# One order of steps over nine token tiles of an attention block: where a tile's last heads and its closing steps stand against the next tile's first ones

## The reference

```
z = rmsnorm(h) @ w_in                       -> cq, ckv, krope, hq, hf, hi, hg
q = rope(rmsnorm(cq) @ w_uq)                8 heads of 64 + 32
s = (q_lat . ckv + q_rope . krope) * SM_SCALE,  chunk-causal mask
o = softmax(s) @ ckv, then w_uv             512 columns (MLA group)
S_t = diag(f_t) S_{t-1} + (1 - f_t) i_t^T,  o_t = S_t^T q_t      4 heads (HGRN2 group)
o_hg = rmsnorm(o_t) * silu(hg)              512 columns
h = h + concat(o_mla, o_hg) @ w_o
h = h + hier_moe(rmsnorm(h));  y = rmsnorm(h)
```

## Time and profile before

| | us |
|---|---|
| median of 3 runs (lowest, highest) | 1440.64 (1438.37, 1443.41) |
| profiled execution, its own time | 1443.98 |
| its span | 1442.0 |
| PE busy in the span | 1180.2 (82%) |
| DVE, ACT, POOL busy | 709.4, 513.3, 327.3 |
| mean granted clock of TensorE | 0.886 of full speed |

### The profile page before, as it was taken

The page is one execution under the profiler, slowest core; times in us unless marked ns, Lnnn a source line. Parts: engine busy times, 40 slices in busy tenths (PEclk is TensorE's granted clock), DMA queues, the critical chain, the costliest instruction groups (busy, mean ns, idle before and its releaser), DMA issues.

```text
span 1442.0 us, 17999 instructions
## 1 busy us (share of the span) xinstructions
PE 1180.2 (82%) x5738; PEld 908.9 (63%) x5738; DVE 709.4 (49%) x1312; ACT 513.3 (36%) x920; POOL 327.3 (23%) x297
## 2 busy tenths in 40 slices
PE   4999999479988988899999999940788998989920
PEld 3898899434757676575757585720566776777720
DVE  4321011254634545454445453441687777778837
ACT  3332121233111112222213232300677777777712
POOL 2101200100000000000000000005565666566546
PEclk9999999769686979989789999975899999999965
DMA  6230211540101201010101000002669686764268
GB/s 231 95 129 23 93 60 48 161 117 20 30 20 44 68 20 59 30 45 30 44 23 51 30 30 23 15 30 65 227 237 345 223 287 221 247 227 151 87 249 310
DMA packets 94042, 160.15 MB, mean 111 GB/s; under 512 B 13435, under 2 KB 62060, under 8 KB 93980
## 3 DMA queue, kind: packets, MB, share of 16 engines
q1 hardware_dynamic: 80460, 114.11, 23.3%
q0 software_dynamic: 12432, 43.14, 8.4%
q10 hardware_dynamic: 1088, 2.10, 0.4%
HBM read 171.69 MB, written 41.10 MB: 148 GB/s over the span
## 4 chain that ended last, share of the span: by engine, by line
PE 59%; issue 11%; DVE 10%; DMA 9%; ACT 6%; POOL 2%; SPq 1%; POOLq 0%; ACTq 0%; DVEq 0%
PE ps L893 9%; DMA below<-in_w 6%; PE ps L861 5%; PE ps L750 4%; PE ps L732 4%; PE ps L820 3%; PE ps L1847 3%; PE ps L1848 3%; PE ps L1849 3%; DVE low L1543 3%; PE ps L1842 2%; PE ps L1841 2%; PE ps L1843 2%; PE ps L792 2%; ACT high L1293 2%
## 5 line engine op out<-in xcount | busy, mean ns | idle before, releaser
L1543 DVE TENSOR_TENSOR low<-below,high 128x1024 fp32r<-128x1024 f32 x132 | 204.1, 1593 | 83.0 <-ACT high L1293 76.5
L1385 PE MATMUL ps<-high 128*128 128x512 f32 x396 | 163.5, 413 | 21.5 <-DVE low L1553 11.3
L1254 POOL TENSOR_TENSOR low<-below,high 128x1024 fp32r<-128x1024 f32 x66 | 152.6, 2332 | 120.3 <-ACT high L1314 120.3
L1717 POOL TENSOR_SCALAR arena<-arena 128x1 f32<-128x1 f32 (+4 forms) x38 | 11.2, 295 | 715.7 <-ACT arena L690 382.1
L517 ACT ACTIVATE arena<-ps 128x512 f32<-128x512 f32 (+7 forms) x109 | 56.9, 531 | 301.9 <-PE ps L732 301.7
L1293 ACT ACTIVATE high<-below 128x1024 fp32r<-128x1024 f32 x132 | 132.9, 1052 | 75.5 <-DMA below<-in_w 75.5
L1387 PE MATMUL ps<-high,low 128*128 128x512 f32 x396 | 157.8, 398 | 0.0
L1386 PE MATMUL ps<-low,high 128*128 128x512 f32 x396 | 157.2, 397 | 0.0
L732 PE MATMUL ps<-arena 128*128 128x128 f32 (+4 forms) x613 | 107.8, 306 | 37.7 <-DVE arena L930 23.8
L893 PE MATMUL ps<-arena 128*128 128x512 f32 (+1 forms) x288 | 125.7, 594 | 2.3 <-ACT arena L517 1.7
L732 PEld LDWEIGHTS ps<-arena 128*128 128x128 f32 (+4 forms) x613 | 84.1, 170 | 53.0 <-issue 32.1
(11 more groups left out here) (209 smaller groups left out, 2035.4 us busy)
## 6 DMA issues: line engine op xcount, KB each, us to landing
below<-in_w SPq DMA_DIRECT2D x264, 256.0 KB
below<-in_w POOLq DMA_DIRECT2D x66, 512.0 KB
y_dram<-arena SPq DMA_DIRECT2D x33, 512.0 KB
arena<-in_x_prompt SPq DMA_DIRECT2D x16, 512.0 KB
below<-in_w_in SPq DMA_DIRECT2D x12, 512.0 KB, 6.4
out<-arena SPq DMA_DIRECT2D x9, 512.0 KB, 5.1
arena<-in_w_o SPq DMA_DIRECT2D x1, 4096.0 KB, 16.9
h_dram<-arena SPq DMA_DIRECT2D x8, 512.0 KB, 2.6
```

The source lines that it names most:

```text
L1254: pool.tensor_tensor(w2_lo[s % UN][:, c], w2_in[:, c], w2_hi[s % UN][:, c].bitcast(F32), ALU.subtract).then_inc(s_w2lo, 1)
L1385: pe.matmul(out, x_hi, w_hi, start=start, stop=False)
L1543: dve.tensor_tensor(chunk(w13_lo[j], c), chunk(w13_in, c), chunk(w13_hi[j], c).bitcast(F32), ALU.subtract).then_inc(s_w13lo, 1)
```

## The change

```diff
-    for i in range(NT):
-        STEPS.append(("meta", i, 0))
+    for i in range(NT + 1):
+        nxt = i + 1 < NT
         for hd in range(MH):
-            STEPS.append(("score", i, hd))
...
-            if hd >= 2:
-                STEPS.append(("attn", i, hd - 2))
-        STEPS += [("attn", i, 6), ("attn", i, 7)]
-        if i + 1 < NT:
-            STEPS.append(("hk", i + 1, 0))
-        STEPS.append(("mpv", i, 0))
...
+            if i < NT:
+                if hd == 0:
+                    STEPS.append(("meta", i, 0))
+                STEPS.append(("score", i, hd))
+                if hd == 0 and i:
+                    STEPS += [("pm", i - 1, 0), ("hk", i, 0)]
+                if hd == 1 and i:
+                    STEPS.append(("ho", i, 0))
+                    if nxt:
+                        STEPS.append(("hs", i + 1, 0))
+                if hd == 2:
+                    STEPS.append(("hf", i, 0))
+            if i and hd == 2:
+                STEPS.append(("mix", i - 1, 0))
+            if i < NT and nxt:
+                STEPS += [("h", i + 1, r) for r in {2: [0], 3: [1], 4: [3]}.get(hd, [])]
+            side = {3: "wot", 4: "wo", 5: "sq", 6: "hn"}.get(hd)
             if i and side:
                 STEPS.append((side, i - 1, 0))
+            if i and hd == 7:
+                STEPS.append(("hnt", i - 1, 0))
+            if i < NT and nxt:
+                STEPS += [("h", i + 1, r) for r in {3: [2], 4: [4], 5: [5], 6: [6], 7: [7]}.get(hd, []) if r < rounds(i + 1)]
+                if hd == 5:
+                    STEPS.append(("q", i + 1, 0))
+                if hd == 7:
+                    STEPS.append(("qt", i + 1, 0))
+            a = i * MH + hd - 2
+            if 0 <= a < NT * MH:
+                STEPS.append(("attn",) + divmod(a, MH))
+            if i and hd == 1:
+                STEPS.append(("mpv", i - 1, 0))
+            if i and hd == 7:
+                STEPS.append(("rt", i - 1, 0))
...
-        if st[0] == "score" and st[2] >= 2:
+        if st[0] == "score" and st[1:] >= (0, 2):
...
     def s_wait_free(pe, st):
         if k >= 2:
             pe.wait_ge(s_srel[k % 2], k // 2)
+            kind, i, _ = S_ORDER[k - 2]
+            if kind == "ho":
+                pe.wait_ge(s_oc, i + 1)
...
-            if kind == "mpv":
+            if kind == "pm":
                 act.wait_ge(s_dm, i + 1)
                 act.activation(pm_row[0:R], pm_row[0:R], ACT.Exp).then_inc(s_pm, 1)
-                evacuate(act, "act", st)
...
                     dve.wait_ge(s_sps2, k + 1)
-                    dve.wait_ge(s_oc, i + 1)
...
+            if kind == "mix":
+                sm = sm_stat[0:R, i % 2]
                 dve.wait_ge(s_pm, i + 1)
```

More of the change, by code:

```diff
@@ L216, in hybrid_layer @@
     pm_row = r.take(MH, META)
-    meta_row = r.take(MH, META)
+    meta_row = r.take(2 * MH, META)
     nbias = r.take(2, MH)
-    sm_stat = r.take(6, MH)
+    sm_stat = r.take(2, 5, MH)
     h_base = r.at
@@ L389, in hybrid_layer @@
     STEPS += [("vm", 0, 0), ("q", 0, 0), ("ho", 0, 0), ("hm", 0, 0), ("hs", 1, 0), ("qt", 0, 0)]
-    for i in range(NT):
-        STEPS.append(("meta", i, 0))
+    for i in range(NT + 1):
+        nxt = i + 1 < NT
         for hd in range(MH):
-            STEPS.append(("score", i, hd))
-            side = {1: "wot", 2: "wo", 3: "sq", 4: "hn", 5: "hnt", 6: "rt"}.get(hd)
-            if hd == 0:
-                STEPS.append(("hf", i, 0))
+            if i == NT and hd == 0:
+                STEPS += [("pm", i - 1, 0)]
+            if i < NT:
[15 more added lines that the diff above has]
+            side = {3: "wot", 4: "wo", 5: "sq", 6: "hn"}.get(hd)
@@ L414, in hybrid_layer @@
-    STEPS += [(s, NT - 1, 0) for s in ("wot", "wo", "sq", "hn", "hnt", "rt")]
+            if i and hd == 7:
[7 more added lines that the diff above has]
+            a = i * MH + hd - 2
@@ L450, in hybrid_layer @@
             P_INDEX[st + (0,)] = len(P_INDEX)
+    S_ORDER = list(S_JOB)
     def last_group(a):
@@ L668, in attention_act @@
             R = ROWS[t]
-            if kind != "mpv":
-                evacuate(act, "act", st)
+            evacuate(act, "act", st)
             if st in S_JOB:
@@ L708, in attention_act @@
                                    bias=nbias[0:R, i % 2, hd:hd + 1], scale=SCALE,
-                                   accum_out=sm_stat[0:R, 2, hd:hd + 1]).then_inc(s_srel[k % 2], 1)
-            if kind == "mpv":
+                                   accum_out=sm_stat[0:R, i % 2, 2, hd:hd + 1]).then_inc(s_srel[k % 2], 1)
+            if kind == "pm":
                 act.wait_ge(s_dm, i + 1)
                 act.activation(pm_row[0:R], pm_row[0:R], ACT.Exp).then_inc(s_pm, 1)
-                evacuate(act, "act", st)
             if kind == "sq":
@@ L943, in attention_dve @@
             R = ROWS[t]
-            if kind != "mpv":
-                evacuate(dve, "dve", st)
+            evacuate(dve, "dve", st)
             if kind == "hs":
@@ L1035, in attention_dve @@
                         dve.wait_ge(s_b7done, B7_JOB[("meta", i, 0)] + 1)
-                        if i:
-                            dve.wait_ge(s_dm, i)
-                        dve.tensor_copy(meta_row[0:R], ps[0:R, 7, 0:MH * META].rearrange("p (h m) -> p h m", h=MH)
+                        mrow = meta_row[0:R, MH * (i % 2):MH * (i % 2) + MH, :]
+                        dve.tensor_copy(mrow, ps[0:R, 7, 0:MH * META].rearrange("p (h m) -> p h m", h=MH)
                                         ).then_inc(s_b7free, 1)
@@ L1041, in attention_dve @@
                         if t == LAST:
-                            link(dve.memset(meta_row[0:SAMPLE], NEG))
-                        dve.tensor_reduce(sm_stat[0:R, 1, :], meta_row[0:R], AX.X, ALU.max)
+                            link(dve.memset(mrow[0:SAMPLE], NEG))
+                        dve.tensor_reduce(sm_stat[0:R, i % 2, 1, :], mrow, AX.X, ALU.max)
                     dve.wait_ge(s_sps2, k + 1)
@@ L1050, in attention_dve @@
                         link(dve.memset(S[0:64, w - 64:w], NEG))
-                    link(dve.tensor_reduce(sm_stat[0:R, 0, hd:hd + 1], S[0:R, 0:w], AX.X, ALU.max))
-                    dve.tensor_scalar(nbias[0:R, i % 2, hd:hd + 1], sm_stat[0:R, 0, hd:hd + 1],
-                                      sm_stat[0:R, 1, hd:hd + 1], -SCALE, ALU.max, ALU.mult).then_inc(s_nb, 1)
+                    link(dve.tensor_reduce(sm_stat[0:R, i % 2, 0, hd:hd + 1], S[0:R, 0:w], AX.X, ALU.max))
+                    dve.tensor_scalar(nbias[0:R, i % 2, hd:hd + 1], sm_stat[0:R, i % 2, 0, hd:hd + 1],
+                                      sm_stat[0:R, i % 2, 1, hd:hd + 1], -SCALE, ALU.max, ALU.mult).then_inc(s_nb, 1)
                 if kind == "wo":
@@ L1062, in attention_dve @@
                                       ALU.add).then_inc(rel, 1)
-            if kind == "mpv":
-                mrow = meta_row[0:R]
+            if kind == "pm":
+                mrow = meta_row[0:R, MH * (i % 2):MH * (i % 2) + MH, :]
                 dve.wait_ge(s_nb, (i + 1) * MH)
@@ L1068, in attention_dve @@
                                          op0=ALU.mult, op1=ALU.add).then_inc(s_dm, 1)
+            if kind == "mix":
+                sm = sm_stat[0:R, i % 2]
                 dve.wait_ge(s_pm, i + 1)
                 s_wait_read(dve, ("score", i, MH - 1))
[L1071 to L1075, removed]
+                link(dve.tensor_reduce(sm[:, 3, :], pm_row[0:R], AX.X, ALU.add))
+                link(dve.tensor_tensor(sm[:, 3, :], sm[:, 3, :], sm[:, 2, :], ALU.add))
+                link(dve.reciprocal(sm[:, 4, :], sm[:, 3, :]))
+                dve.wait_ge(s_pused, P_INDEX[("mpv", i, 0, 0)] + 1)
                 dve.tensor_tensor(mix_row[0:R, :].rearrange("p (h v) -> p h v", h=MH),
                                   ps[0:R, 6, :].rearrange("p (h v) -> p h v", h=MH),
-                                  sm_stat[0:R, 4, :].unsqueeze(2).to_broadcast([R, MH, VD]), ALU.mult
+                                  sm[:, 4, :].unsqueeze(2).to_broadcast([R, MH, VD]), ALU.mult
                                   ).then_inc(s_mix, 1)
```

## The result

The changed kernel takes 1460.39 us (median of 4 runs, 1455.28 to 1461.99) against 1439.51 us (4 runs): ratio 1.0134, 95% interval 1.0102 to 1.0167. I had forecast 1431 with a range to 1452. The result lies on the other side of no change, and beyond the range.

A forecast was written before the change was run, and what follows sets the result against it. PE was taken to bound the attention: work at the upper clock, the lower clock's price, and waiting. Walked at full clock -22 us, +12 for the lower clock, +0.5, makes -10: forecast 1431 us, range 1412 to 1452.

The forecast's parts named there:

- The walked waits: PE's new waits in the attention, walked at full clock for i = 7 (9.8 us) and i = 3 (some 12).
- the mix: At i = 7 the new tile's first product waits 2.7 us for s_mix, behind score2, hf and the sums on DVE.
- `attn7`'s copy: attn7's product waits for DVE's copy, 2.0 us at i = 7, or ACT's behind the squares, 1.8 at i = 3.
- bank 7: At i = 3, h'1 waits 2.9 us for this bank, because DVE frees it behind hf and mix.
- `h'2`: This round waits for DVE's h'1, which stands behind score3: 1.7 us at i = 7; 1.5 at i = 3.
- step 3: After ho at i = 7: DVE's state, hs' and attn7 first-group copy take 3.1 us, cover 1.1, wait 2.0.
- `ho` for the first exponential: At i = 3, ho waits 1.6 us for head 0's exponential, which holds its slot, behind pm and hk on ACT.
- `hk`'s bank: At i = 7, the second group of attn6 waits 1.8 us for the bank that ACT's copy of hk frees.
- What the lower clock will cost: Attention: 12 us, between 0 and 22; two waits a tile cost 5 us of slower work, 3.5 of it absorbed.
- the first tile: Its rounds begin two heads later: +1 us, called small.
- the long runs of transposes: attn5 to attn7 held the clock down for 20 us and more in narrow tiles; scores and ho break them up.
- The third: Rival: rt and meta back to back ahead of score0 keep the clock down through ho; +36 us, 1455 us, chance 0.26.

The follow-up runs named there:

- qt_early: Kernel before with one step moved, the next tile's qt ahead of attn6 and attn7: 1405.5 us, ratio 0.9763 to before.
- mix_and_pm: Changed kernel with mix directly behind mpv and pm behind the tile's last maxima: 1437.7 us, ratio 0.9993 to before.
- mpv_spread: Order of qt_early in the changed kernel's code, pm behind attn5, mpv between attn6 and attn7, its last products and mix behind hk: 1392.6 us, ratio 0.9659 to before.
- experiment 1: Changed kernel with the router product rt moved from ahead of meta to behind mpv in the tile after: 1458.9 us, ratio 1.0126 to before.
- Experiment 7: qt_early with a wait put back at meta, for ACT's copy of ho, ACT's squares or POOL's power: 1425.7, 1437.8 and 1453.2 us.
- score0_ahead: mpv_spread with the next tile's meta and score0 moved ahead of this tile's attn7: 1437.7 us, ratio 1.0005 to before.

## Why the prediction was wrong

**Right: what goes and what comes.** The wait of meta went. The walked waits came, in place and roughly in size: the mix 2.7 forecast, 2.39 in tile i = 7 (2.1 to 3.4 in the four wide tiles); `attn7`'s copy 2.0 and 1.8, measured 1.2 to 2.0 (0.4 in the last tile); bank 7 in the narrow tiles 2.9, measured 2.2 to 2.6 (in the fourth 1.2); `h'2` 1.7, measured 0.5 to 1.4. Two sums of the walk were loose: the waits listed for i = 3 add up to 13.0 us ("some 12"), and the chain of step 3 to 2.9 ("3.1"); neither changes the forecast by more than 4 us. Too large were those that a PE at the lower clock reaches late: `ho` for the first exponential (1.6, once 0.8) and `hk`'s bank (1.8, at most 0.95).

**The step that failed: "What the lower clock will cost ... I take 12".** At full clock the walk gave -22 us for the tiles. The stretch came out at +15.9. That leaves 38 us for the lower clock and the first tile where the sum had 12 + 0.5. About 29 of them are the term that I had put at 12. My 12 was eight tiles of 5 us of slower work less 3.5 us that the waits absorb, so 40 less 28. What the windows give for the same two parts, as an estimate: PE is busy for 477 us in the eight windows with 411 us of work at full clock (my 417, less the 6 us done earlier), so 66 us of slower work; the walk had 93 us of waiting at full clock (510 less 417) and 56 are idle, so 37 absorbed. The waits absorbed somewhat more than I took. The slower work did not: it was 67 us before and stayed there, where I had it fall to 40.

I had argued that the long runs of transposes held the clock down and that breaking them up frees it. In sum nothing was freed: the busy time of the stretch is 524.6 us against 521.9. In the narrow tiles the breaking up may have helped (i = 2 went from 0.81 to 0.94), and the wide ones gave it back. From tile i = 4 on the runs were not the cause: in `qt_early` the runs of `attn5` to `attn7` stand as before, `qt` among them, and from 569 us to the end of the last `attn` the clock falls once, for 3 us. What frees it there is that the wait ahead of meta is gone: one put back at the same place brings back some 20 of the 29 us of busy time, in each of three profiles. The changed kernel has two or three waits of over 1 us in each tile's start but the last's. That each of them has such a price is argued from this; the runs that took some of them out got back less than meta's price (`mix_and_pm`: 12.0 us of idle and 5.3 us of busy time). Why the first two tiles are at the lower level for most of their time in every order, `mpv_spread` too (0.71 from 361 to 440 us), no run shows.

**Also mis-sized: the first tile.** I gave "+1" for its rounds beginning later. From the first meta record to the first product of meta probabilities it takes 53.9 us against 39.0 (360.19 to 399.22). Some 6 us of this is work that the new order does earlier; the rest, about 9, is loss: idle 8.6 us instead of 3.5, at a clock of 0.69.

**The rivals.** The third ("the lower clock through the tile's start", 1455) had the side, and with 36 us nearly the size. Its cause, `rt` and `meta` back to back, found no support: with `rt` elsewhere nothing was gained (experiment 1). That its time came close is luck. It should have been put on the waits, of which I had already counted more than before. Seen from the rule of the Trainium skill that I had weighed ("TensorE: Matmul & The Clock Gate", "HAM oscillation — how this bites in real kernels"), reading it as the forecast would have given the right side. The section behind it, "A second HAM failure mode: psum-queue depth-cycling", fits these runs closer: it says that short idle moments between groups of matmuls, if frequent, make the clock go up and down as well. Its case is a bf16 kernel with 512 columns. Experiment 7 agrees in part: eight waits of 0.7 us cost 19 us of busy time in the profiled execution, and three of four executions paid about that. Frequent they are not, one in each tile of 57 to 70 us.

**What the forecast hid.** The change does two things. The queries' move is worth 34 us (`qt_early` against before, 1405.5 and 1439.5). The rest, `hk`, `ho`, `mpv` and `mix` under the next tile, costs 55 (1460.4 less 1405.5); no single run makes this step alone, so it is a difference and not a measurement. In a sum of waits at full clock the two looked like -22; neither waits alone nor the clock alone give their sizes.

**Open.** Why the step in busy time sits at this place is not settled: `qt_early` keeps waits of 1.0 us at round 0 and of up to 1.7 us in narrow tiles with much of its time at full clock, while 0.7 us directly ahead of meta costs 19 us. Nor is it meta alone. `qt_early` waits 0.75 us ahead of `mpv`'s product (L745) in all the tiles from the second on, and in three of them the product's two records then run at the lower level, as here:

```profile
763.75 2.08 PE L745 MATMUL ps<-arena 128*128 128x512 f32 x2 [0.75 <-DVE arena L551]
```

In four others they take 1.13 us behind the same wait. `mpv_spread`, in which these waits are covered, has no lower stretch from 498 us on. So the same wait at the same place has a price at one time and none at another, and what decides it these runs do not show. That the 16-column products of meta matter is an idea that no run here tests apart.

## What to carry to other kernels

Before work is moved ahead of a wait, ask what it was covering where it stood: here `ho`, meta and score0 covered DVE's chains, and where they had stood waits of about 2 us came (round 0 in `score0_ahead`, the mix and `attn7` in the changed kernel), even where the wait that they went to fill was gone already. Price a wait of TensorE by an experiment that adds one, since the clock can make it worth three times its length (5.9 us of waiting, 20 us of time in experiment 7); a sum of waits at full clock can have the wrong sign. And move one step at a time: one line of this change was worth 2.4%, the whole of it was a loss.

## What the runs showed of the hardware

The price of waiting looks like a step: eight waits of 0.7, 2.0 or 3.7 us on average at the same place raise the busy time of the same 2652 records from 492 us to 512, 515 and 511, one profile each. It is not always paid: with the shortest wait one execution of four ran at the clock of the kernel without it (0.916) and was 14 to 16 us faster than the other three. Between the best order and the changed kernel's (`mpv_spread`, 34 us idle; changed, 66 us idle) TensorE is busy for 485 and 525 us with identical work, at mean granted clocks of 0.94 and 0.88: more than half of the difference in time is not in any gap.
